# Softmax weights of two attention branches transposed by DMA instead of the tensor engine, with a moved schedule

## The reference

```python
for l in range(DEPTH):                                   # 2
    xn = _rms_norm(x, attn_norm_g[l])
    (...) = jnp.split(xn @ w_in[l], split_at, axis=-1)
    o_a = _stick_breaking(...)                           # A, 4 heads of 64
    o_b = ... _diff_attention(...)                       # B, two softmax maps a head
    o_c = _moba(mq, mk, _heads(mb_v))                    # C, block-sparse
    o_d = _nsa(nq, ns_kc, ns_vc, ns_ks, ns_vs, ns_kw, ns_vw, g_nsa, ...)   # D, three paths
    for i, o in enumerate((o_a, o_b, o_c, o_d)):
        g = jax.nn.sigmoid(xn @ w_gate[l, i] + b_gate[l, i])
        term = g * (_merge_heads(o) @ w_branch[l, i])
        merged = term if merged is None else merged + term
    x = x + merged @ w_out[l]
    hn = _rms_norm(x, ffn_norm_g[l])
    x = x + (silu(hn @ w_ffn_gate[l]) * (hn @ w_ffn_up[l])) @ w_ffn_down[l]
```

## Time and profile before

| what | value |
|---|---|
| median of 3 runs | 836.74 us |
| profiled execution | 836.82 us, span 834.6 us |
| granted TensorE clock | 1.000 of full speed |
| PE busy | 829.7 us (99%) |
| DVE, ACT, POOL busy | 555.9, 465.8, 263.5 us |
| DMA queue of SP | 162.07 MB, 62.0% of 16 engines |

### The profile page before, as it was taken

The page is one execution under the profiler, slowest core; times in us unless marked ns, Lnnn a source line. Parts: engine busy times, 40 slices in busy tenths (PEclk is TensorE's granted clock), DMA queues, the critical chain, the costliest instruction groups (busy, mean ns, idle before and its releaser), DMA issues.

```text
span 834.6 us, 11178 instructions
## 1 busy us (share of the span) xinstructions
PE 829.7 (99%) x4122; PEld 681.1 (82%) x4122; DVE 555.9 (67%) x821; ACT 465.8 (56%) x715; POOL 263.5 (32%) x273
## 2 busy tenths in 40 slices
PE   9999999999999999999999999999999999999998
PEld 6888888878888888888888888887888888888886
DVE  5576888757866666655454688887587666666542
ACT  6886655665455545543457775547544654554441
POOL 0078773004303333320000889530052034233100
PEclk9999999999999999999999999999999999999999
DMA  9745674454548777785565466745535588777752
GB/s 328 270 142 187 204 227 152 152 181 162 201 166 230 218 210 222 219 223 183 168 216 185 151 202 188 222 143 180 189 138 200 188 218 227 223 210 217 218 180 74
DMA packets 100822, 163.06 MB, mean 195 GB/s; under 512 B 37792, under 2 KB 40224, under 8 KB 100512
## 3 DMA queue, kind: packets, MB, share of 16 engines
q1 hardware_dynamic: 100480, 162.07, 62.0%
q10 hardware_dynamic: 288, 0.27, 0.1%
HBM read 153.40 MB, written 1.05 MB: 185 GB/s over the span
## 4 chain that ended last, share of the span: by engine, by line
PE 98%; DMA 1%; issue 0%; SPq 0%; ACT 0%; DVE 0%
PE acc L721 90%; PE att L801 1%; PE att L883 1%; PE att L768 1%; PE att L858 1%; DMA w_raw<-in_w_in 1%; PE att L874 1%; PE att L793 1%; PE acc L801 0%; PE acc L858 0%; PE att L842 0%; PE att L896 0%; PE att L960 0%; PE att L951 0%; PE att L843 0%
## 5 line engine op out<-in xcount | busy, mean ns | idle before, releaser
L1214 DVE TENSOR_TENSOR w_lo<-w_raw,w_hi 128x1024 fp32r<-128x1024 f32 (+1 forms) x276 | 363.7, 1330 | 154.4 <-ACT w_hi L984 151.7
L721 PE MATMUL acc<-w_hi,xt 128*128 128x512 f32 (+1 forms) x1728 | 433.5, 393 | 0.5 <-ACT xt L1007 0.5
L984 ACT ACTIVATE w_hi<-w_raw 128x1024 fp32r<-128x1024 f32 (+1 forms) x275 | 286.7, 1052 | 170.5 <-PE acc L721 164.8
L721 PEld LDWEIGHTS acc<-w_hi,xt 128*128 128x128 f32 x1728 | 318.2, 188 | 65.1 <-ACT w_hi L984 0.9
L721 PE MATMUL acc<-w_lo,xt 128*128 128x512 f32 (+1 forms) x864 | 229.8, 388 | 0.0
L721 PEld LDWEIGHTS acc<-w_lo,xt 128*128 128x128 f32 x864 | 162.0, 188 | 32.9
L1465 POOL TENSOR_SCALAR small<-small 128x2 f32<-128x2 f32 (+4 forms) x14 | 9.3, 664 | 209.9 <-ACT sq_dump L1084 132.4
L1593 POOL TENSOR_TENSOR merged<-merged,prod 128x1024 f32<-128x1024 f32 x10 | 32.4, 3243 | 128.4 <-DVE prod L1263 127.6
L1576 POOL COPY hid_halves<-hid 128x512 uint16<-128x512 uint16 x44 | 45.6, 1064 | 66.7 <-DVE hid L1291 66.7
L1585 POOL COPY hid_t<-hid_halves_t 128x512 uint16<-128x512 uint16 x44 | 35.3, 831 | 95.2 <-DMA hid_halves_t<-hid_halves 80.8
L721 PE MATMUL acc<-w_hi,ht_hi 128*128 128x512 f32 x176 | 47.7, 390 | 0.0
(11 more groups left out here) (179 smaller groups left out, 697.7 us busy)
## 6 DMA issues: line engine op xcount, KB each, us to landing
w_raw<-in_w_ffn SPq DMA_DIRECT2D x88, 512.0 KB, 3.9
w_raw<-in_w_gate SPq DMA_DIRECT2D x64, 512.0 KB, 3.3
w_raw<-in_w_ffn_down SPq DMA_DIRECT2D x44, 512.0 KB, 4.0
w_raw<-in_w_in SPq DMA_DIRECT2D x39, 512.0 KB, 4.8
w_raw<-in_w_branch SPq DMA_DIRECT2D x16, 512.0 KB, 3.3
w_raw<-in_w_out SPq DMA_DIRECT2D x16, 512.0 KB, 3.2
bg<-in_b_gate SPq DMA_DIRECT2D x8, 512.0 KB, 5.4
w_raw<-in_w_in SPq DMA_DIRECT2D x8, 396.0 KB, 3.6
```

The source lines that it names most:

```text
L721: return pe.matmul(acc[bank0 + t][:, 0:N], x_part[:, k0 + k, t * P:(t + 1) * P], w_part[:, k, 0:N], start=first, stop=last)
L984: act.activation(w_hi[:, n % WR, :, 0:N], w_raw[:, n % RAW, :, 0:N], copy).then_inc(s_hi, 1)
L1214: dve.tensor_tensor(w_lo[:, n % WR, :, 0:N], w_raw[:, n % RAW, :, 0:N], w_hi[:, n % WR, :, 0:N].bitcast(F32), ALU.subtract).then_inc(s_lo, 1)
```

## The change

The twelve maps of C and D are transposed by DMA. `pt` of C and D goes, and with it `aside` (the use of a free projection bank for every second one). In its place stand `pdeal` on POOL (each of a pair's two maps dealt into half-words, 768 of them, once `p` is done), `turn_p` on SP (one DMA transpose of 12 blocks a pair, at the six chunks of `TURN_P`, with two buffers in turn, laid over the part of `proj` that A's and B's inputs have left), and `pjoin` on ACT (two copies of 768 half-words into `ptb`). The products with v wait for `pjoin` instead of the `pt` copies, and the exponential buffers come free with `pdeal`. From a pair's third use on, `pdeal` waits until the transpose two pairs back has landed, and `turn_p` until the join two pairs back is done.

The table is moved with it: C's products with v from chunk 41 to 46, D's first scores and scalings from 41 to 42, D's first products from 49 to 52, the compressed product from 45 to 51, B's norm from 38 to 40, and the output steps of B and C from 44 to 45 and 48. The FFN is the same in both, with x as the stationary side.

```diff
+TURNS = [("C", 0), ("C", 1), ("D", 0), ("D", 1), ("D", 2), ("D", 3)]
+TURN_P = (43, 47, 52, 53, 55, 56)
...
-    "Cdeal": 24, "Cjoin": 30, "Csm": (35, 35), "Cp": (35, 38), "Cpt": (38, 38, 39, 39), "Cpv": (41, 41), "Dc": 27,
+    "Cdeal": 24, "Cjoin": 30, "Csm": (35, 35), "Cp": (35, 38), "Cpdeal": (36, 39), "Cpjoin": (41, 45), "Cpv": (46, 46), "Dc": 27,
...
-    "Dpt": (45, 45, 46, 47, 50, 51, 53, 54), "Dpv": (49, 49, 57, 57),
+    "Dpdeal": (43, 43, 47, 48), "Dpjoin": (49, 50, 53, 54), "Dpv": (52, 52, 57, 57),
...
+            def turn_p(l, step):
+                k = TURNS.index(step)
+                sp.wait_ge(pdealt.sem, pdealt.at(l, ("pdeal", step)))
+                if k > 1:
+                    sp.wait_ge(pjoined.sem, pjoined.at(l, ("pjoin", TURNS[k - 2])))
+                sp.dma_start_transpose(p_halves_t[k % 2][:, :, :, :].rearrange("p i s (b q) -> p (i s b) q", q=P),
+                                       p_halves[k % 2][:, :, :, :].rearrange("p i s c -> p (i s c)")
+                                       ).then_inc(s_pturn[k % 2], 16)
...
+                    if u in TURN_P:
+                        turn_p(l, TURNS[TURN_P.index(u)])
...
             def times_v(l, step):
                 mixer, m = step[1]
-                src = {"A": ("cum", m), "B": ("pt", (mixer, m))}.get(mixer, ("pt", (mixer, 2 * m + 1)))
-                pe.wait_ge(read_act.sem, read_act.at(l, src))
+                src = {"A": ("cum", m), "B": ("pt", (mixer, m))}.get(mixer, ("pjoin", (mixer, m)))
+                ev = pjoined if src[0] == "pjoin" else read_act
+                pe.wait_ge(ev.sem, ev.at(l, src))
...
+                elif kind == "pjoin":
+                    k = TURNS.index(a)
+                    act.wait_ge(s_pturn[k % 2], p_turned(l, a))
+                    pb = pt_free(l, step)
+                    for i in range(2):
+                        ins = act.activation(ptb[:, pb + i, :].bitcast(U16).rearrange("p (c s) -> p s c", s=2),
+                                             p_halves_t[k % 2][:, i, :, :], copy)
+                    ins.then_inc(pjoined.now(step), 1)
...
+                        elif kind == "pdeal":
+                            k = TURNS.index(a)
+                            pool.wait_ge(dve_misc.sem, dve_misc.at(l, ("p", a)))
+                            if k > 1:
+                                pool.wait_ge(s_pturn[k % 2], p_turned(l, TURNS[k - 2]))
+                            elif k == 1:
+                                pool.wait_ge(att_done.sem, att_done.at(l, ("pv", ("B", PAIRS["B"] - 1))))
+                            for i in range(2):
+                                e = e_of(("sm", a))[0][i]
+                                ins = pool.tensor_copy(p_halves[k % 2][:, i, :, :],
+                                                       e_map(e).bitcast(U16).rearrange("p (c s) -> p s c", s=2))
+                            ins.then_inc(pdealt.now(step), 1)
```

More of the change, by code:

```diff
@@ L160, in steps @@
         for n in range(PAIRS[mixer]):
-            for kind in {"A": ("z", "sp", "cum", "pv"), "B": ("p",)}.get(mixer, ("p", "pv")):
+            for kind in {"A": ("z", "sp", "cum", "pv"), "B": ("p",)}.get(mixer, ("p", "pdeal", "pjoin", "pv")):
                 put(PLAN[mixer + kind][n], kind, n if mixer == "A" and kind != "pv" else (mixer, n))
         for m in range(MAPS[mixer]):
-            for kind in ("pt", "pv") if mixer == "B" else ("pt",):
+            for kind in ("pt", "pv"):
                 put(PLAN[mixer + kind][m], kind, (mixer, m))
@@ L258 @@
 SLOT = {s: u for u in range(NCH + 1) for s in STEPS[u]}
-def aside(step):
-    kind, a = step
-    return kind == "pt" and a[0] != "B" and a[1] % 2 == 1 and SLOT[step] % 4 != 0 and SLOT[step] < U_BR
 def result_at(u):
@@ L270, in result_at @@
     return RESULTS.index({"in": ("proj", a), "gate": ("zg", a)}[kind])
-IDLE_USES = [s for s in ORDER if second(s) or aside(s)]
+IDLE_USES = [s for s in ORDER if second(s)]
 IDLE_OF = {s: RESULTS[result_at(SLOT[s]) + 1] for s in IDLE_USES}
@@ L278, in banks_of @@
     kind, a = step
-    if second(step) or aside(step):
+    if second(step):
         return (IDLE,)
@@ L315, in e_of @@
     first = 4 + 2 * n if mixer == "D" and n < 2 else 2 * (n % 2)
-    return (first, first + 1), ("pt", (mixer, n if mixer == "B" else 2 * n + 1))
+    return (first, first + 1), ("pt" if mixer == "B" else "pdeal", (mixer, n))
 E_STEPS = [s for s in ORDER if s[0] in ("z", "sm")]
@@ L324, in pt_slots @@
     kind, a = step
-    return (2 * a, 2 * a + 1) if kind == "cum" else (a[1] % 4,)
-PT_USES = [[s for s in ORDER if s[0] in ("cum", "pt") and slot in pt_slots(s)] for slot in range(4)]
+    if kind == "pjoin":
+        return 2 * (a[1] % 2), 2 * (a[1] % 2) + 1
+    return (2 * a, 2 * a + 1) if kind == "cum" else (a[1],)
+PT_USES = [[s for s in ORDER if s[0] in ("cum", "pt", "pjoin") and slot in pt_slots(s)] for slot in range(4)]
 def pv_step(s):
@@ L365, in trunk_kernel @@
         proj = place("proj", [P, NT, IN_COLS], F32)
+        p_halves, p_halves_t = ([place(f"{name}{i}", [P, 2, 2, 384], U16, at=big + t * (4 * IN_COLS + 16) + 12 * i * MIX)
+                                 for i in range(2)] for t, name in enumerate(("p_halves", "p_halves_t")))
         zg = place("zg", [P, NT, 4, D_MODEL], F32)
@@ L500, in trunk_kernel @@
         s_turn = sem("halves_transposed")
+        pdealt = Events(sem("p_halves_dealt"), keys("pdeal"))
+        pjoined = Events(sem("p_joined"), keys("pjoin"))
+        s_pturn = [sem(f"p_halves_transposed{i}") for i in range(2)]
         s_hturn = [sem(f"hid_halves_transposed{i}") for i in range(2)]
@@ L557, in e_free @@
                 if prev:
-                    engine.wait_ge(att_done.sem, att_done.at(prev[0], e_of(prev[1])[1]))
+                    free = e_of(prev[1])[1]
+                    ev = pdealt if free[0] == "pdeal" else att_done
+                    engine.wait_ge(ev.sem, ev.at(prev[0], free))
         def e_map(e):
             return eb[:, e, :] if e < 4 else eb_more[:, e - 4, :]
-        def pt_bank(l, step):
-            return acc[bank_pair(l, IDLE_OF[step])] if aside(step) else att[:, TP, :]
         def score_bank(l, step, i):
@@ L1111, in do @@
                     pb = pt_free(l, step)
-                    act.activation(ptb[:, pb, :], pt_bank(l, step)[:, 0:384], copy).then_inc(read_act.now(step), 1)
+                    act.activation(ptb[:, pb, :], att[:, TP, 0:384], copy).then_inc(read_act.now(step), 1)
+                elif kind == "pjoin":
[6 more added lines that the diff above has]
+                    ins.then_inc(pjoined.now(step), 1)
                 elif kind == "cpt":
```

22 lines of the change are left out of this document (11 added, 11 removed).

## The result

The changed kernel takes 828.06 us (median of 4 runs, 827.63 to 828.20), the kernel before, run beside it, 836.52 (836.25 to 837.12). The ratio is 0.9897, with a 95% interval of 0.988 to 0.9914. So it is faster, by 8.5 us or 1.0%. The profiled execution took 828.20, its span being 826.4. That leaves 1.8 us around the span, where it was 2.2. Where the remaining 0.9 us came from is the question of what follows.

A forecast was written before the change was run, and what follows sets the result against it. PE, never idle, was taken to bound the kernel; 72 transposes and their restarts leaving it were worth 7.8 us (between 7.7 and 8.1), so 836.82 - 7.8 = 829.0 us, range for 8 in 10 from 828.2 to 832.

The forecast's parts named there:

- The bound: Whole kernel: PE, busy 99% of the span with waits of 1.2 and 0.5 us only, sets the time by its matmuls.
- The places: Layer 0: D's first scores at about 139.7, second 154.6, D's products with v 173.4, D's pair 1 joined at 171.5.
- So any step between two chunks costs 0.10 for the restart as well: On PE, eight products behind three transposes take 1.93 us, not 1.83; six interruptions fewer give 0.6 us a layer.
- The upper bound 72 x 0.113: On PE, 72 removed transposes at 113 ns each, (0.24 + 0.10) / 3, give 8.1 us from above.
- The 2.2 us around it stay.: Outside the span: profiled execution 836.82 us against a span of 834.6; the 2.2 us between were to remain.
- The likeliest case's low end: Low end, 828.2 us, of the forecast's own range of 828.2 to 830; this case had chance 0.76.
- Costs of the path: POOL, DMA, ACT: deals 1.8 to 4.8 us a pair, landing 5.7 (3.3 to 10.2), joins 1.6 a pair.
- Rival 2: POOL's copies block DVE, delaying w_lo, the weights' low part; 1 to 2 us a layer, 831 to 833; chance 0.06.
- the rule: A DVE instruction with two SBUF inputs contends with a GpSimd one reading SBUF; each new copy could hold up a w_lo.
- Rival 4: On PE: the change doesn't free it, because something else is just as close; chance 0.02.
- Rivals 1: A join on ACT comes late for PE, most likely D's pair 1; 2 to 3 us a layer at worst, 830 to 834; chance 0.12.
- Rival 3: 12-block DMA transpose far slower than 8 blocks suggest; landing at chunk 52 has 16 us; slower than before, 845; chance 0.04.

## Why the prediction came out as it did

**The bound.** Right. PE sets the time before and after, and the span follows the sum of its starts. No other engine comes in, with POOL at 21.2 and DVE at 40.2 of 45 us.

**The places.** Right within about 0.1 us: D's first scores at 139.7 (139.72), the second at 154.6 (154.52), D with v at 173.4 (173.51), D's pair 1 joined at 171.5 (171.50). The chain through the moved steps could be worked out from before's rows alone, since PE never waits. The join's time, unlike PE's, is right by luck: see the costs of the path below.

**"So any step between two chunks costs 0.10 for the restart as well."** This step failed in size: 0.12. Twelve of them are 0.24 us. With the six transposes behind compressed matmuls (0.61 and 0.64 instead of 0.58) and roundings the groups give 0.11 a layer more. I then took 7.8 between 7.7 and 8.1, since most groups stand alone, and the stream gave 8.16. The upper bound 72 x 0.113 was no bound: it took 0.10 too, and without the restart it has six in a row at 0.48, where they took 0.58 to 0.64. That it equals 8.1 all the same is because it charges 24 restarts for the 12 that went.

**"The 2.2 us around it stay."** This failed: 1.8. I had nothing for it but that it is the same kernel. It should have been a term with a spread of its own. These two together are 0.36 + 0.4 = 0.76 of the 0.94 us between forecast and median; of the other 0.18, 0.14 is the median lying below the profiled execution, from whose time before I had started; the runs scatter over 0.6 us.

**The likeliest case's low end was too near.** 828.2 stood 0.8 us below the forecast, with two terms unmeasured whose joint error was that large.

**Costs of the path.** Landing 5.0 us at the median, 6.6 at worst (taken 5.7, range 3.3 to 10.2). Deals 1.6 to 3.5 us a pair (1.8 to 4.8). A pair's join takes 1.99, not 1.6: I had scaled 384 elements at 0.49, and 768 half-words with a stride take 1.06, the time of a conversion of 1024. That pair 1's join still ended at 171.5 is luck. By the starts of ACT's rows above, the exponentials ended at 160.26 (160.3). Three conversions and C's step, up to 163.58, took 3.32 us where I had 3.75, and the fourth conversion, from 168.71, 0.94 for 1.05: 0.54 less. Pair 0's join with the sigmoid behind it took 5.13 for 4.8, and pair 1's join 1.85 for 1.6: 0.58 more. The two errors cancel. ACT's busy time rose by 12.0 us, 6.0 a layer, where I had counted 3.7: the joins are dearer. That the window from 120 to 165 rose by 3.68 is chance, as it holds only part of the joins.

**Rival 2 and the rule.** I looked for the collision at w_lo, as an instruction with two inputs. w_lo does stretch (1.23 to 2.60 at most), but the scaling stretches more in proportion (0.32 to 0.91), and the earlier trace rows had shown only POOL's side. The scalings' line for the other exponential buffer in the kernel before would have told me, with its maximum of 1.25 us against a median of 0.34. The slowest starts at 533.98, beside a copy on POOL from 533.92 to 535.08:

```profile
L1377 DVE TENSOR_SCALAR eb<-eb,small x32: 276/336/1248, 121.0 to 579.5; 128x128 f32<-128x128 f32 x16, 128x256 f32<-128x256 f32 x16
```

The Trainium skill (SBUF — State Buffer, "Who interferes with whom") has it as well: beside the two-input case that I used it lists `tensor_scalar` among the operations that can take the port shared with GpSimd. By that rule the rows of the three kernels agree, with medians of 0.32, 0.34 and 0.73 us as POOL's copies come in and double.

**Not separated.** Rival 4 is out (8.16 us left PE). Rivals 1 and 2 exist, each beginning within a doubling of its cause. Rival 3, a landing that holds up PE, was not reached: SP's queue gave way first, and the 16 us that I gave a landing at chunk 52 stay untested.

## What to carry to other kernels

Where one engine is never idle, price an edit by the starts of its groups in the trace, and count interruptions apart from their content: here a first transpose costs 0.14 with its restart and each further one 0.11, so steps that share one gap save 0.1 us each. When work leaves the bound engine, everything behind it is asked for sooner, and the next step may run into a buffer still being read; moving it back costs nothing if something else has left the same gap. A margin of 2 us on such an engine can be worth more than 2 us: here a wait of 1.9 us was followed by another 1.6 us lost at half the clock. And a forecast closer than half a microsecond has to price what lies outside the span.

## What the chip showed that I had not expected

- A wait of 1.9 us, on a TensorE that had been busy throughout, was followed by about 3.4 us at half the granted clock (0.50 in the window 177 to 179), which nearly doubled its price. The waits of 0.2 to 0.9 us in the traces of the other kernels went without it, with a granted clock of 0.999 to 1.0 over the span. Two of this kernel's ten runs list a full clock and took as long, which is open.
- A longer program on POOL, by 32 waits that never wait, shortens the run by 0.4 us outside the span, and the fetch of instructions behind the last instruction goes with it. That the one is the cause of the other is not shown.
- DVE's scaling with one SBUF input tile goes from 0.32 to as much as 0.91 us beside POOL (1.25 in one case of the kernel before), more in proportion than w_lo with two.
- ACT takes 1.06 us for 768 strided half-words, as long as for 1024 elements converted from 32 bits.
